# Attention phase: transposes and value products three units behind the scores instead of two, value products in two parts, the ratio of the weights from one tensor operand

## The reference, cut to what matters

```python
def diff_combine(s, lam):
    p = jax.nn.softmax(s, axis=-1)
    return p[..., 0, :, :] - lam * p[..., 1, :, :]

# prompt, 8 heads, query blocks of 128 rows, causal
s = jnp.einsum('bqhmd,bkhmd->bhmqk', qi, k) * ATTN_SCALE     # two score maps per head
s = jnp.where(k_pos[None, :] <= q_pos[:, None], s, NEG)
return jnp.einsum('bhqk,bkhe->bqhe', diff_combine(s, lam), v)

# samples: the same over 8 pages of 128 cached keys each, and the new key
k_past = cache_k[page_table]
s_past = jnp.einsum('bqhmd,bkhmd->bhmqk', q, k_past) * ATTN_SCALE
```

## Time and profile before

| | us |
|---|---|
| median of 3 runs | 4176.69 (4170.09 to 4177.06) |
| the profiled execution | 4166.23, its span 4164.5 |
| attention phase in the span | 2593 to 3206 |
| mean granted TensorE clock | 0.896 of full speed |

### The profile page before, as it was taken

One profiled execution on the slowest core, in us unless ns is written; L12 is line 12 of the kernel. 1 busy time (PEld: TensorE's weight loads), 2 busy tenths in 40 slices (PEclk: granted clock), 3 DMA queues, 4 the chain that ended last, 5 costly groups with the idle time before them and its releaser, 6 DMA issues. The chain is left out here.

```text
span 4164.5 us, 78261 instructions
## 1 busy us (share of the span) xinstructions
PE 3483.6 (84%) x34038; PEld 3147.2 (76%) x34038; DVE 1899.8 (46%) x2159; ACT 1346.4 (32%) x2059; POOL 1563.1 (38%) x648
## 2 busy tenths in 40 slices
PE   5889686898897298999999999455775989999896
PEld 2888435888786188999999998333443889999896
DVE  3333606455542586353454430677433772522622
ACT  1111113433432134333333433333444333333332
POOL 0111000000000155656656665455000656556563
PEclk8999858999998599999999999667887999999998
DMA  5222123334331543445444665545353534444442
GB/s 191 83 85 73 46 92 126 122 113 149 114 105 48 167 124 115 133 131 152 141 138 140 183 188 158 193 152 202 137 202 102 163 104 139 127 138 140 125 141 71
DMA packets 710476, 546.83 MB, mean 131 GB/s; under 512 B 34763, under 2 KB 667491, under 8 KB 709885
## 3 DMA queue, kind: packets, MB, share of 16 engines
q1 hardware_dynamic: 664182, 473.18, 36.9%
q10 hardware_dynamic: 45606, 67.55, 4.7%
q0 software_dynamic: 352, 1.18, 0.1%
HBM read 471.55 MB, written 70.29 MB: 130 GB/s over the span
## 5 line engine op out<-in xcount | busy, mean ns | idle before, releaser
L1630 POOL TENSOR_TENSOR dense_w_lo<-dense_w_raw,dense_w_hi 128x1024 fp32r<-128x1024 f32 x504 | 1273.4, 2532 | 974.8 <-ACT dense_w_hi L1701 974.6
L1686 PE MATMUL acc<-dense_x_hi,dense_w_hi 128*128 128x344 f32 x2496 | 813.2, 330 | 86.2 <-DVE dense_x_lo L1791 41.4
L1687 PE MATMUL acc<-dense_x_lo,dense_w_hi 128*128 128x344 f32 x2496 | 802.3, 326 | 0.0
L1701 ACT ACTIVATE dense_w_hi<-dense_w_raw 128x1024 fp32r<-128x1024 f32 x504 | 531.1, 1056 | 628.8 <-PE acc L1691 536.0
L1686 PEld LDWEIGHTS acc<-dense_x_hi,dense_w_hi 128*128 128x128 f32 x2496 | 482.4, 193 | 98.6 <-issue 79.7
L1687 PEld LDWEIGHTS acc<-dense_x_lo,dense_w_hi 128*128 128x128 f32 x2496 | 482.6, 193 | 2.5 <-issue 0.9
L1686 PE MATMUL acc<-dense_hid_hi,dense_w_hi 128*128 128x344 f32 x1536 | 483.4, 319 | 0.5 <-DVE dense_hid_lo L1811 0.5
L1687 PE MATMUL acc<-dense_hid_lo,dense_w_hi 128*128 128x344 f32 x1536 | 483.4, 319 | 0.0
L1691 PE MATMUL acc<-dense_x_hi,dense_w_lo 128*128 128x344 f32 x2496 | 449.7, 323 | 1.3 <-POOL dense_w_lo L1630 1.3
L1691 PEld LDWEIGHTS acc<-dense_x_hi,dense_w_lo 128*128 128x128 f32 x2496 | 409.9, 190 | 2.1 <-POOL dense_w_lo L1630 1.8
L750 POOL TENSOR_TENSOR x0T<-nT,levels 128x512 f32<-128x512 f32 x16 | 29.7, 1855 | 744.0 <-DVE bR L1249 744.0
(11 more groups left out here) (384 smaller groups left out, 5983.6 us busy)
## 6 DMA issues: line engine op xcount, KB each, us to landing
dense_w_raw<-in_ffn_w SPq DMA_DIRECT2D x384, 512.0 KB, 4.1
ada_quarter<-in_ada_w SPq DMA_DIRECT2D x40, 1024.0 KB, 11.0
att_k_page<-in_cache_k SPq DMA_DIRECT2D x64, 512.0 KB, 3.6
att_v_page<-in_cache_v SPq DMA_DIRECT2D x64, 512.0 KB, 5.9
scratch_mix<-proj_stage ACTq DMA_DIRECT2D x48, 516.0 KB, 2.7
scratch_mix<-dense_stage ACTq DMA_DIRECT2D x72, 172.0 KB, 2.1
w_raw<-in_a_w_rkv SPq DMA_DIRECT2D x24, 512.0 KB, 4.2
dense_w_raw<-in_a_w_o SPq DMA_DIRECT2D x24, 512.0 KB, 4.5
```

The costliest lines, as they stand in the source:

```text
L1630: nc.gpsimd.tensor_tensor(wlo[:, i % NW], raw[:, i % NRAW], whi[:, i % NW].bitcast(F32), ALU.subtract).then_inc(S("lo"), 1)
L1686: T_.matmul(out, whi[:, s % NW, k, :], a, start=j.first and k == 0, stop=False)
L1687: T_.matmul(out, whi[:, s % NW, k, :], b, start=False, stop=False)
L1701: A(whi[:, i % NW], raw[:, i % NRAW], ACT.Copy).then_inc(S("hi"), 1)
```

## The change

Six edits, all in `attention_phase`:
1. The transposes and value products at unit u are those of w = u - 3 (`LAG`). For it the combinations get two buffers per kind (`attn_of`) and the small per-row numbers four.
2. `values` comes in two parts of up to 4 blocks. For a long unit the first part stands behind the second round of transposes, then one extra, then the second part, then the other extras. For a short unit one extra stands ahead of the values.
3. The ratio is a `tensor_scalar` of the reciprocal with two per-row scalars, in place of a `scalar_tensor_tensor` that reads two tensors.
4. GpSimd's products have three buffers (`NR`): product j may start when page sum j - 3 is done.
5. The scores of unit 0 come before the transposes of the sample columns; those go to other banks one after the other, and SP loads mask, keys and queries first, the page table later.
6. The per-head steps on GpSimd, VectorE and ScalarE move by one unit.

```diff
-        NK, NV = 4, 12
+        NK, NV, NR = 4, 12, 3
-        END = NU + 10
+        END, LAG = NU + 10, 3
-        at = (sb("attn_long", [P, SEQ]), sb("attn_short", [P, SEQ // 2]))
+        at = (sb("attn_long", [P, 2, SEQ]), sb("attn_short", [P, 2, SEQ // 2]))
-        mx, nb, l, rl, w1 = (sb(x, [P, 2, 2]) for x in ("max", "neg_max", "sums", "weights", "ratio"))
+        mx, nb, l, rl, w1 = (sb(x, [P, 4, 2]) for x in ("max", "neg_max", "sums", "weights", "ratio"))
...
+        def attn_of(u):
+            return at[kind(u)][:, (u // 2) % 2]
...
-                        need(pool, "red", j - 1)
-                        nc.gpsimd.tensor_tensor(prod[:, j % 2, :], kp[:, j % NK, :], qb[:, b % 2, :], ALU.mult).then_inc(S("prod"), 1)
-                if u % KC == 2 and u > 2:
+                    need(pool, "red", j - NR + 1)
+                    nc.gpsimd.tensor_tensor(prod[:, j % NR, :], kp[:, j % NK, :], qb[:, b % 2, :], ALU.mult).then_inc(S("prod"), 1)
+                if u % KC == 3 and u > 3:
...
-            def values(w):
+            def values(w, part):
                 h, n = w // KC, blocks(w)
-                need(pe, "take", w)
-                need(pe, "t_in", nth["rows", h, 3] + 1)
-                for j in range(n):
-                    if j % 4 == 0:
-                        need(pe, "t_in", nth["attn", w, j // 4] + 1)
+                if part == 0:
+                    need(pe, "take", w)
+                    need(pe, "t_in", nth["rows", h, 3] + 1)
+                need(pe, "t_in", nth["attn", w, part] + 1)
+                for j in range(4 * part, min(n, 4 * part + 4)):
                     last = T_.matmul(ob[:, 0:P], aT[kind(w)][:, j * P:(j + 1) * P], vrow[:, h % 2, j, :],
                                      start=(j == 0), stop=(j == n - 1))
...
+            need(pe, "consts", 2)
+            need(pe, "in_k", 16)
+            scores(0)
             pe.wait_ge(S("cols_in"), 48)
...
             for u in range(END):
-                w = u - 2
+                w = u - LAG
                 live = 0 <= w < NU
                 if live:
                     need(pe, "attn", w + 1)
...
-                if u < NU:
+                if 0 < u < NU:
                     scores(u)
+                todo = extras(u)
                 if live and blocks(w) > 4:
-                    turn4(("attn", w, 1), [at[kind(w)][:, j * P:j * P + P] for j in range(4, blocks(w))])
-                for name in extras(u):
+                    turn4(("attn", w, 1), [attn_of(w)[:, j * P:j * P + P] for j in range(4, blocks(w))])
+                    values(w, 0)
+                elif live and todo:
+                    extra(todo.pop(0))
+                    values(w, 0)
+                elif live:
+                    values(w, 0)
+                if live and blocks(w) > 4:
+                    if todo:
+                        extra(todo.pop(0))
+                    values(w, 1)
+                for name in todo:
                     extra(name)
-                if live:
-                    values(w)
...
-                need(dve, "take", u - 1)
+                need(dve, "take", u - 3)
...
-                V.scalar_tensor_tensor(w1[:, kd, 0:1], rl[:, kd, 1:2], lam[:, 0:1], l[:, kd, 0:1], ALU.mult, ALU.mult).then_inc(S("ratio"), 1)
+                V.tensor_scalar(w1[:, c, 0:1], rl[:, c, 1:2], l[:, c, 0:1], lam[:, 0:1], ALU.mult, ALU.mult).then_inc(S("ratio"), 1)
                 need(dve, "ratio", u + 1)
-                if u >= 2:
-                    need(dve, "t_mm", nth[attn_rounds(u - 2)[-1]] + 1)
+                if u >= 4:
+                    need(dve, "t_mm", nth[attn_rounds(u - 4)[-1]] + 1)
```

More of the change, by code:

```diff
@@ L1933, in kind, with pages_of @@
             return u % 2
+        def attn_of(u):
+            return at[kind(u)][:, (u // 2) % 2]
+        def pages_of(u):
+            return range(min(NPAGE, 2 * u), min(NPAGE, 2 * u + 2))
         def sample_of(u):
@@ L1984, in attention_phase @@
         nth = {}
-        for name in [("rows", 0, i) for i in range(4)] + [n for u in range(END) for n in attn_rounds(u - 2) + extras(u)]:
+        for name in [("rows", 0, i) for i in range(4)] + [n for u in range(END) for n in attn_rounds(u - LAG) + extras(u)]:
             nth[name] = len(nth)
@@ L2041, in _ @@
                     nc.sync.dma_start(v[:], m.scr[S_V, h + 1, :, 0:SEQ]).then_inc(S("in_v"), 16)
[L2042 to L2046, removed]
+                for j in pages_of(u + NK // 2):
+                    k_page(j)
+                    if j % NP == NP - 2 and 1 < j // NP + 1 < NS:
+                        q_row(j // NP + 1)
                 if u == KU - 8:
@@ L2166, in extra, with sample_turn @@
                 last.then_inc(S("t_mm"), 1)
-            pe.wait_ge(S("cols_in"), 48)
[L2169 to L2173, removed]
+            def sample_turn(t, banks):
+                for h in range(NH):
+                    last = T_.transpose(banks[0:NS, h // 4, (h % 4) * P:(h % 4 + 1) * P], t[:, h, :], m.ident[:])
+                last.then_inc(S("qkv_t"), 1)
+            need(pe, "consts", 2)
+            need(pe, "in_k", 16)
+            scores(0)
+            pe.wait_ge(S("cols_in"), 48)
+            sample_turn(qs, six[:, 4:6, :])
+            sample_turn(ks, m.aux2)
+            need(pe, "sample_rows", 1)
+            sample_turn(vs, six[:, 4:6, :])
+            need(pe, "sample_rows", 2)
             need(pe, "consts", 4)
@@ L2256, in _ @@
                     maxima(u)
-                if u < KU:
-                    page_sums(2 * u)
+                todo = list(pages_of(u))
+                if todo:
+                    page_sums(todo.pop(0))
                 if 1 <= u <= NU:
                     combine(u - 1)
-                if u < KU:
-                    page_sums(2 * u + 1)
-                if r == 3 and 1 <= h <= NH:
+                for j in todo:
+                    page_sums(j)
+                if r == 4 and 1 <= h <= NH:
                     need(dve, "osq", h)
@@ L2317, in _ @@
             A(ls[:], ls[:], ACT.Exp).then_inc(S("lam_exp"), 1)
-            need(act, "qkv_t", 1)
-            for i in range(3):
-                A(rows[:, i, :].rearrange("p (a n) -> p a n", a=2), (m.acc[0], m.acc[1], m.aux2)[i][0:NS, 0:2, :],
-                  ACT.Copy).then_inc(S("sample_rows"), 1)
+            for i, banks in enumerate((six[:, 4:6, :], m.aux2, six[:, 4:6, :])):
+                need(act, "qkv_t", i + 1)
+                A(rows[:, i, :].rearrange("p (a n) -> p a n", a=2), banks[0:NS], ACT.Copy).then_inc(S("sample_rows"), 1)
             def head_rows(h, part):
```

51 lines of the change are left out of this document (26 added, 25 removed).

## The result

The changed kernel takes 4101.0 us (median of 4 runs, 4096.3 to 4107.2) against 4173.4 for the kernel before in the same job: ratio 0.983, 95% interval 0.981 to 0.985. The profiled execution took 4096.3 us.

The account below looks back on a forecast made before the run. In stage one no engine was full: VectorE and TensorE took turns in a closed loop. Terms 38 + 18 + 3 = 59 us gave 4107 from the profiled execution, 4118 from the median; forecast 4113 us, range 4075 to 4150.

Parts of the forecast that it names:

- Lag of three: Stage one (units 1 to 31): VectorE's 66.3 us wait for scores should go; 38 us gained, range 15 to 55.
- the 8.2 us: Stage one: forecast length of one VectorE unit, against 9.65 us before.
- The 7 us set aside for a late TensorE: Stage one: 7 us taken off the 45 for TensorE running late at head turns and after long score rows.
- Ratio from one operand, priced at nothing: Stage one: the wait for GpSimd's product passes from ratio to combination; 0 us, where the row alone promised 46.
- The end of the combination doesn't move: Stage one: the combination behind a ratio that no longer waits meets the same GpSimd product, so nothing is gained.
- Negation at 1.3 us in the mean: Stage one: sign that VectorE's negated maximum, waiting for GpSimd's product, takes near 1.3 us in the mean.
- Third buffer at nothing: Stage one: GpSimd is still released by a page sum at the same point of VectorE's unit; 0 us.
- Value products in two parts: Stage two (units 32 to 63): value products hide transpose-bank hand-overs; 18 of 42 us, TensorE's unused time near 40.
- Prologue: Start of the phase: unit 0's scores before the sample transposes; 3 us gained, bounds 1 us slower to 5 gained.
- Tail: End of the phase: TensorE has one more unit to transpose and multiply after the last scores; 0, at worst 3 us.
- TensorE and ScalarE binding stage one: Rival: with hand-overs stage one takes 9.4 us a unit and gives only 8 us; 4142 us, chance 0.13.
- clock rival: Two rivals on TensorE's granted clock: stage two's rises, 4093 or 4085 us, chance 0.13; it falls, 4198, chance 0.04.

Follow-up runs that it names:

- two-operand ratio: Changed kernel with the ratio of weights again reading two tensor operands: 4121.1 us, ratio 0.989 to the kernel before.
- The run with the order alone: Kernel before with only the value products in two parts between the other transposes: 4150.5 against 4168.5 us, ratio 0.995.
- short products: Changed kernel with GpSimd multiplying only the first 64 of each key page's 1024 columns, only to measure: 4032.6 us.
- values last: Changed kernel with both parts of a unit's value products behind all other transposes again: 4120.4 us, ratio 0.990 to the kernel before.
- half products: Changed kernel with each GpSimd product of a key page made as two instructions of 512 columns: 4061.9 us, ratio 0.975 to the kernel before.
- negation by columns: Changed kernel with the negated maximum made as two instructions of one number per partition: 4059.8 us, ratio 0.973 to the kernel before.
- both: Changed kernel with products in two instructions of 512 columns and the negated maximum in two of one number: 4047.8 us, ratio 0.970 to the kernel before.

## Why the prediction was right, and where its sizes were off

It said 4113 us, measured 4101; against the profiled time the sum was 59 us and 70 came.

- **Lag of three.** Right in mechanism: VectorE's wait for scores vanished, and with a lag of two it is back. Stage one gave 58.4 where the term was 38. The run with the two-operand ratio splits the 58.4: all other edits together give 42.1 (299.1 to 257.0), close to the 38, and the ratio's operand, which the sum had at nothing, the other 16.3 (257.0 to 240.7). (The shares depend on the order; the lag undone by itself costs 48.5.) Seen by units, the 8.2 us were close, as the two middle heads take 64.5 us, 8.07 a unit, extras of the head included. Three things made up the 20 between 38 and 58. The 7 us set aside for a late TensorE weren't needed (0.5 us of waiting). The first eight units take 58.0 us instead of 64.5, and the last one, with no product beside it, 4.88 instead of 8.07: 9.7 together, where the sum took 31 equal units. And 31 x (8.2 - 8.07) = 4.
- **Ratio from one operand, priced at nothing.** This step failed. "The end of the combination doesn't move" is wrong by 0.25 us in nearly every unit and by 1.84 once a head, where GpSimd's square stands next in its queue; undone, the edit costs 16 us of stage one. What held is that the row by itself (46 us) can't be had: the combination took over nearly all of the wait. In the kernel before the edit is indeed worth nothing in time. The 38 hid this: its unit was worked out with the wait moved already, but the combination's own time counted in full behind the product, 1.15 us at 896 columns where 0.96 was measured.
- **Negation at 1.3 us in the mean.** 1.07, with up to 2.33, as the unit's steps had it; by columns it is free.
- **Third buffer at nothing.** So it measured in stage one as a whole (241.2 with two, 240.7 with three), though the first eight units gain 3 us and each middle head loses 1.4.
- **Value products in two parts.** 18 against 13.4 in the trace, and the number came out better than the mechanism. The 18 were to be hand-overs, with TensorE's unused time near 40 us afterwards. It is 52.0, against 55.6 before: only some 4 of the 13.4. The rest is TensorE's busy time, 204.4 to 194.0, with 17 instructions fewer in the stage and a clock of 0.83 instead of 0.82. The run with the order alone shows why: it gives 20 (259.7 to 239.6), 10.6 of them hand-overs and 9.4 at a higher granted clock, which the term didn't contain; and the lag's own cost to stage two (unused time of 52 and 53 us in the changed kernel's two traces, 45 and 46 with a lag of two) was missing from the working. The large wait did stay (15.2 us before, 26.6 now, at the long units instead).
- **Prologue.** 3 against 0.3, when the heads before and after are compared (30.0 and 29.7). Undone on the changed kernel it is worth 1.6 in the head and 3.5 in the first eight units, so 5 in the trace; by time it isn't told apart from nothing. The first product starts 23.8 us into the phase instead of 20.7; the prologue's edit accounts for 1.7 of this, just the 1.7 taken for late sample rows (22.1 without it), and the other 1.4 has no cause shown.
- **Tail.** 0 against 1.7, in seven of the nine later kernels with a lag of three 5.4, outside the "at worst 3".
- **Rivals.** TensorE and ScalarE binding stage one is excluded by the short products. The clock hardly moved in stage two (0.82 or 0.83 before; 0.83 and 0.85 in the two traces after) and rose in stage one (0.69 to 0.73), so neither clock rival came. But it isn't inert: values last had 0.78, and to forecast it as unchanged was in part luck.

On the lock the Trainium skill (SBUF — State Buffer, section "SBUF: two separate sides") says that whoever starts first keeps the shared ports for its whole instruction; half products agree with it, as the wait shrank with the instruction. The Trainium skill (VectorE: DVE Perf Modes, section "What auto-detection actually checks") names as the condition of the two-port mode a single source and the destination in SBUF "with outermost non-unit dims both even or equal"; the negation of [P, 2], held at 1065 ns, agrees with that. What the rule makes of [P, 1], which has no such dimension, it doesn't say; that the negation is free there, at 149 ns, is what the run shows.

## What to carry to other kernels

Where two engines take turns in a loop, one more unit of lag on the consumer turns their sum into a maximum; check with the wait view that the other engine's wait is what it removed. Then look at what the bound engine is busy with: an instruction of one or two numbers that takes microseconds is a wait in disguise, and moving it saves only a part of it (16 of 46 us here), but another operand shape or a shorter instruction on the engine that it waits for does. Price a wait that moves by the gap behind it too: what stands next in the other engine's queue decides who goes first.

## What the runs showed of the hardware that was not expected

- The negation, a `tensor_scalar`, waited for GpSimd's product up to 2.33 us in one instruction of 2 numbers per partition, and never in two of 1 number (62 of 62 at 149 ns mean). The count alone doesn't decide it: the reciprocal of 2 numbers never waited, and the ratio of 1 number did when it read two tensors (2283 ns mean in stage one of the ratio of two tensors, 220 ns in stage two of the kernel before).
- GpSimd waits in turn when VectorE is first. In the changed kernel both instructions started at 2722.13, and the product took 3.43 us instead of 2.35, 1.08 of the VectorE instruction's 1.22 us on top:

```profile
2722.13 1.22 DVE L2297 TENSOR_TENSOR att_o<-att_o,att_rms 128x1024 f32<-128x1024 f32 x1
2722.13 3.43 POOL L2077 TENSOR_TENSOR att_k_prod<-att_k_page,att_q_row_all 128x1024 f32<-128x1024 f32 x1 [2.09 <-DVE att_scores L2274]
```

- Stage two, in which GpSimd makes no products, took 238 to 241 us in four kernels with a lag of three (negation by columns, half products, both, ratio of two tensors), at a clock of 0.86 to 0.88, and 244 to 246 in the changed kernel, at 0.85 and 0.83. It is the same work again: in the negation by columns 187.3 us busy x 0.87 = 163. A shorter stage one isn't the reason, as short products has the shortest (176.9) and stays at 245.4 and 0.84, and the ratio of two tensors has a longer one (257.0). What sets the clock there is open.
